# The place of the conditioning blocks in the first feed-forward stage, and who scales the last result

## What is computed

```python
def swiglu(x, w_gate_up, w_down):
    gate, up = jnp.split(x @ w_gate_up, 2, axis=-1)
    return (jax.nn.silu(gate) * up) @ w_down

# first block, for each of two layers
x = x + 0.5 * swiglu(rms_norm(x, ffn1_norm[l]), ffn1_w_gate_up[l], ffn1_w_down[l])
...                                      # three mixers
x = x + 0.5 * swiglu(rms_norm(x, ffn2_norm[l]), ffn2_w_gate_up[l], ffn2_w_down[l])

# second block
mod = silu(c) @ w_ada[l] + b_ada[l]      # 1024 x 6144, the conditioning
...
x = x + gt2 * ((silu(gte) * val) @ w_down[l])
return rmsnorm(x, g_final)
```

## Time and profile before

| what | value |
|---|---|
| time, median of 3 runs | 1635.75 us (1634.82 to 1635.97) |
| profiled execution, its own time | 1637.86 us |
| its span, first to last instruction | 1635.9 us |
| PE busy | 1583.6 us, 97% of the span |
| DVE, ACT, POOL busy | 80%, 62%, 24% |
| chain that ended last | PE 76%, DVE 13%, ACT 6%, DMA 2%, issue 2% |
| mean granted clock of PE | 0.98 of full speed |

### The profile page before, as it was taken

The page is one execution under the profiler, slowest core; times in us unless marked ns, Lnnn a source line. Parts: engine busy times, 40 slices in busy tenths (PEclk is TensorE's granted clock), DMA queues, the critical chain, the costliest instruction groups (busy, mean ns, idle before and its releaser), DMA issues.

```text
span 1635.9 us, 33829 instructions
## 1 busy us (share of the span) xinstructions
PE 1583.6 (97%) x14144; PEld 1452.6 (89%) x14144; DVE 1304.3 (80%) x2149; ACT 1011.4 (62%) x1852; POOL 394.6 (24%) x304
## 2 busy tenths in 40 slices
PE   9999998999999999999999899999999999889997
PEld 7888998988898888888899898889888899889987
DVE  6888678977868886788767997876987677889964
ACT  5775458667457764677445877646775557566742
POOL 1674000000106740277200000011773100211110
PEclk9999999999899999999999999899999999989998
DMA  7675643512266656566563341245665643245442
GB/s 270 248 267 187 217 137 92 148 49 80 104 249 235 232 202 209 205 260 225 193 227 97 112 122 36 80 155 205 236 259 178 217 161 141 104 155 185 177 160 97
DMA packets 97128, 282.77 MB, mean 173 GB/s; under 512 B 7760, under 2 KB 61648, under 8 KB 73936
## 3 DMA queue, kind: packets, MB, share of 16 engines
q1 hardware_dynamic: 96256, 279.48, 48.5%
q10 hardware_dynamic: 720, 1.13, 0.2%
HBM read 279.53 MB, written 1.05 MB: 172 GB/s over the span
## 4 chain that ended last, share of the span: by engine, by line
PE 76%; DVE 13%; ACT 6%; DMA 2%; issue 2%; POOL 0%; ACTq 0%; DVEq 0%; POOLq 0%
PE banks L516 25%; PE banks L517 13%; PE banks L508 7%; PE banks L509 7%; PE banks L510 7%; PE banks L1836 3%; DVE WL L479 3%; PE banks L1188 2%; PE banks L1190 2%; PE banks L1189 2%; DMA ring<-wst 2%; ACT ring L800 1%; ACT WH L474 1%; PE banks L1845 1%; DVE ringr L1143 1%
## 5 line engine op out<-in xcount | busy, mean ns | idle before, releaser
L479 DVE TENSOR_TENSOR WL<-ring,WH 128x2048 fp32r<-128x2048 f32 (+1 forms) x218 | 457.6, 2110 | 103.6 <-ACT WH L474 103.5
L516 PE MATMUL banks<-XNP,WH 128*128 128x512 f32 x1408 | 496.1, 396 | 3.4 <-DVE XNP L610 2.2
L474 ACT ACTIVATE WH<-ring 128x2048 fp32r<-128x2048 f32 (+1 forms) x222 | 378.7, 1714 | 46.1 <-PE banks L510 40.2
L517 PE MATMUL banks<-XNP,WL 128*128 128x256 f32 x1408 | 393.3, 279 | 0.0
L516 PEld LDWEIGHTS banks<-XNP,WH 128*128 128x128 f32 x1408 | 264.0, 187 | 64.5 <-DVE XNP L610 3.3
L1029 POOL TENSOR_TENSOR HP<-G,HP 128x256 fp32r<-128x256 f32 x110 | 210.4, 1913 | 300.9 <-ACT HP L820 300.9
L516 PE MATMUL banks<-HP,WH 128*128 128x512 f32 x770 | 269.1, 394 | 2.6 <-DVE G L932 1.8
L517 PEld LDWEIGHTS banks<-XNP,WL 128*128 128x128 f32 x1408 | 265.6, 189 | 0.0
L517 PE MATMUL banks<-HP,WL 128*128 128x256 f32 x770 | 215.9, 280 | 0.0
L516 PEld LDWEIGHTS banks<-HP,WH 128*128 128x128 f32 x770 | 145.3, 189 | 35.6 <-DVE G L932 2.1
L517 PEld LDWEIGHTS banks<-HP,WL 128*128 128x128 f32 x770 | 145.3, 189 | 0.0
(11 more groups left out here) (543 smaller groups left out, 4031.7 us busy)
## 6 DMA issues: line engine op xcount, KB each, us to landing
ring<-wst SPq DMA_DIRECT2D x179, 1024.0 KB, 4.9
ring<-wst SPq DMA_DIRECT2D x80, 704.0 KB, 4.0
ring<-wst SPq DMA_DIRECT2D x108, 256.0 KB, 2.9
LP<-lp SPq DMA_DIRECT2D x1, 1872.0 KB, 7.1
LP<-lp SPq DMA_DIRECT2D x4, 448.0 KB, 5.7
X<-xin ACTq DMA_DIRECT2D x4, 256.0 KB, 7.9
out<-X SPq DMA_DIRECT2D x4, 256.0 KB, 2.2
C<-cst SPq DMA_DIRECT2D x1, 193.0 KB, 4.8
```

Source lines behind the costliest of these rows:

```text
L474: e.do.activation(WH[:, slot[q], 0:n], ring[:, slot_at(i), 0:n], ACT.Copy).then_inc(*w_act.up("high", q))
L479: e.do.tensor_tensor(WL[:, slot[q], 0:n], ring[:, slot_at(i), 0:n], WH[:, slot[q], 0:n].bitcast(F32), ALU.subtract).then_inc(*w_dve.up("lo ...
L516: e.do.matmul(b[:, :], WH[:, s, cols], x.rearrange("p s t -> p (s t)"), start=first, stop=False)
L517: return e.do.matmul(b[:, 0:T], WL[:, s, cols], x[:, 0, :], start=False, stop=last)
```

## The change

The last three conditioning blocks of stage 0 stand behind the tiles 15, 17 and 19 instead of 16, 19 and 21. All loads behind them in the list shift accordingly, as do ACT's and POOL's steps for these blocks (steps 12, 14, 16 instead of 13, 16, 18), PE's transposes and DVE's sums; no sum of stage 0 is left in the down part. In stage 4 ACT writes each finished tile, scaled with the final scale, into `X` behind its square, and DVE forms the result from that in four instructions of two tiles each instead of eight of one tile, each behind a wait for ACT's scaled tiles.

```diff
 def ada_up(f):
-    return (7, 10, 13, 16, 19, 21) if f == 0 else (5, 8, 11, 14, 17, 20)
+    return (7, 10, 13, 15, 17, 19) if f == 0 else (5, 8, 11, 14, 17, 20)
...
                         e.do.activation(SQ[:, n % 2, :], src[:, n, :], ACT.Square).then_inc(*f_act.up("sq", f, n))
+                        if f == 4:
+                            e.do.activation(X[:, n, :], X2[:, n, :], ACT.Copy, scale=spc("gfin", n)).then_inc(*f_act.up("scaled", n))
...
             e.wait_ge(*b_pe.on("rows", "end"))
-            for k in range(KT):
-                e.do.scalar_tensor_tensor(X[:, k, :], X2[:, k, :], spc("gfin", k), bank[7][:, 0:T], ALU.mult, ALU.mult).then_inc(*b_dve.up("result", k))
+            for k in range(0, KT, 2):
+                e.wait_ge(*f_act.on("scaled", k + 1))
+                e.do.tensor_tensor(X[:, k:k + 2, :], X[:, k:k + 2, :], bank[7][:, 0:T].unsqueeze(1).to_broadcast([128, 2, T]), ALU.mult).then_inc(
+                    *b_dve.up("result", k + 1))
```

## The result

| what | before | after |
|---|---|---|
| median, runs of both in turn | 1635.8 us (20 runs) | 1637.84 us (20 runs, 1634.92 to 1640.82) |
| ratio after / before | | 1.0013, 95% interval 1.0007 to 1.0019 |
| profiled execution, its own time | 1637.86 us | 1636.07 us |
| its span | 1635.9 us | 1633.8 us |

The account below looks back on a forecast made before the run. PE, busy 97% of the span, was taken as the bound. 1637.86 + 1.1 (moved blocks) - 0.6 (result) gave 1638.4 us of own time; the +0.5 us carried to the median gave 1636.2 us, range 1634.2 to 1638.9.

Parts of the forecast that it names:

- What bounds it: Whole kernel: PE is busy 97% of the span; stage 0's stall and slow clock before the down part hold 3.5 us.
- the loops: Stage 0, blocks 2 to 5: three slot loops of 13.33 us against 11.48 us of PE work, 4.4 us of stalls.
- Part 1: Moved blocks in stage 0: down part 2.79 us later, less 1.7 us of slow clock, so +1.1 us.
- Part 2: Result at the kernel's end: four products in 2.49 us instead of 3.22, gaining 0.2 to 0.73 us, taken as 0.6.
- carrying the difference over to the median: Whole kernel: the +0.5 us found against the profiled execution was added to the timed runs' median, giving 1636.2 us.
- The sum: Whole kernel: 1637.86 + 1.1 - 0.6 = 1638.4 us of the profiled execution's own time, +0.5 us.
- The first rival: Stage 0: slow clock loss no longer hidden, or absent from earlier timed runs; 1.7 us added, 1637.9 us; 22%.
- Works as said: Stage 0 and end: blocks end earlier, PE never waits, stall and slow clock gone, end shorter; 1631.6 us; 8%.
- Loads of 7.01 us: Stage 0: three conditioning loads take 7.01 us instead of 4.84, each loop grows by 2.17; 1642.7 us; 7%.

Follow-up runs that it names:

- e3: The changed kernel with only 64 of 2048 columns loaded for conditioning blocks 3 to 5 of stage 0; 1638.22 us in one execution.
- e1: The changed kernel with the result formed as before, so only the blocks of stage 0 moved; 1640.51 us, ratio 1.0017 to the kernel before.
- e2: The changed kernel with the blocks of stage 0 placed as before, so only the new result form; 1636.59 us, ratio 0.9998 to the kernel before.
- e11: The changed kernel with the blocks of stage 0 behind tiles 7, 9, 12, 15, 18, 21; 1636.57 us, ratio 0.9997 to the kernel before.
- before_again: The kernel before, unchanged, profiled once more for its trace; stage 0 took 187.22 us.
- e10: The changed kernel with the blocks of stage 0 behind tiles 6, 9, 12, 15, 18, 21; 1636.49 us, ratio 0.9995 to the kernel before.
- e8: The changed kernel with ACT's block scaling ahead of tanh and hidden-value rounding in steps 12, 14, 16 of stage 0; 1644.65 us in one execution.

## Why the prediction was right or wrong

**What bounds it, and the loops: right in the numbers, half right in the reason.** Forecast for the scalings of blocks 3 to 5: 93.59, 106.92, 120.25; seen 93.48, 106.69, 119.89. Forecast for the waits 0.74 + 1.85 + 1.85 = 4.44 us; seen 1.15 + 1.42 + 1.62 = 4.2. Down part forecast at 141.96, seen at 141.75. But ACT didn't stand idle for the loads of blocks 4 and 5. Two loops of one length ran beside each other (block 4's load landed less than 0.1 us before its scaling began), and I had priced one. e3 shows that the other gives 13.1 us by itself. In the forecast this did no harm, because they are equal; whoever had mended the loads on its strength would have gained little.

**Part 1 against the profiled execution: right.** Forecast +1.1 us; stage 0 took 188.84 against 187.82, +1.0.

**Part 2: right.** Forecast -0.6; the four products take 2.48 us (forecast 2.49), the stores land after 2.4 us instead of 2.2, and the way from the last square to the end is about 0.5 us shorter. The Trainium skill (VectorE: DVE Perf Modes, The TRN2 errata — SBUF-src ops pay a fixed extra latency per instruction) would put a product at an estimated 658 ns, four at 2.63 us, a gain of 0.59 us (not the 0.56 of the prediction). The trace has 0.68 us for one product and 2.48 for four, since each starts 0.60 us behind the one before, and the row was the better guide. The scaled copies are hidden, the last one ending at 1625.41, 3 us ahead of the products.

**The step that failed: carrying the difference over to the median.** "That execution lies 2.1 us above the median of the timed runs, so I carry the difference of +0.5 us over to the median." The sum credited the change with 1.7 us of slow clock that would no longer be lost. The earlier trace rows were read rightly, but they were one execution, and three of four traces of this stage don't lose it. Against those three (mean 186.97 us) the changed stage 0 is 1.9 us longer, and with 0.5 us back from part 2 the sum is +1.4; the measurement says 2.0 (1.1 to 3.1). The first rival named this condition ("the timed runs of before were without the drop that the profile shows") and its time, 1637.9, against 1637.84 measured. It came out so close partly by luck: without the drop before gains not 1.7 us but about 0.85 (187.82 - 186.97), because the wait of 1.1 us for POOL in the down part, which no row of the first profile could show, then takes some of it back (the first wait differs between the traces as well, 0.8 to 1.8 us). That the timed runs are mostly without the drop is inferred: three of four traces lack it, and the timed runs, which have no trace, have a mean granted clock of 0.983 (median of the 27 beside e1 and e2) where the profiled execution has 0.980, which doesn't say where the clock fell. The 0.6 us between the sum and the measurement are open and within its interval.

The hint stood there: the profiled execution's own time was 2.1 us above the median. I wrote that down and still used a loss seen in it alone.

**The other rivals.** "Works as said" (1631.6) fell with the loops. Loads of 7.01 us didn't come in after: the three landed 4.7 to 4.9 us after their issue. But such loads do come where distances are three tiles (e11), so the mechanism was real at another place.

## What to carry to other kernels

Before crediting an edit with a stall, look at more than one trace of the kernel before: a slow clock in one execution is neither sure to return nor free of cover, since it can hide the next wait. When a loop's length fits one chain of waits, look at what the timeline puts ahead of the repeating instruction; here two chains of 13 us ran side by side, and mending either alone gave little or did harm. Moving work earlier in a ring costs where the distances become shorter than the loop, and at the start where the work isn't ready yet.

## What the runs showed of the hardware that was not expected

Three up tiles of stage 0 take PE different times, though its list of waits names none among them. Stretches between two pairs of transposes, at granted clock 1.00, in before_again and in e10:

```profile
108.71:125.20 16.49, 16.49 (x97) 14.41 (x96) 14.15 (x15) 12.52 (x20) 11.84 (x7) 1.00 0.66 235
```

```profile
104.04:121.20 17.16, 17.05 (x97) 14.82 (x97) 14.78 (x17) 11.97 (x21) 11.69 (x8) 1.00 0.70 243
```

That is 0.67 us more for as much work, and e10 has it twice. Half of it is a wait after all, of the weight loads (PEld). These are listed apart from PE's matmuls, and in e10 they wait twice for DVE's low weights, 0.35 us before tile 16 and 0.30 before tile 19, while in before_again they don't wait here:

```profile
PEld banks L516 <- DVE WL L479: 0.7, 2, 0.3
```

Of such a wait only 0.11 us shows as idle time of PE in the stretch, because PE still has the transposes in hand; but the first matmul starts 0.49 us behind them (104.15) instead of 0.14. So in e10 the low weights come a little late even at distances of three tiles. The other half is a rhythm: in PE's timeline the pairs of matmuls follow each other at some 353 ns on average in this stretch of e10, at 347 in before_again, which makes 0.3 us over three tiles. Both rhythms occur in the traces of before as well (its three tiles take 16.87 or 17.18 us with their transposes). What sets the rhythm was not tried. Added up over stage 0, the slower pairs cost between 0.4 and 1.6 us in the thirteen traces (0.9 in before_again, 1.4 in e10), so it moves the stage by up to about 1 us, as much as half of the difference that was to be explained.

A wait of a given length doesn't decide the clock by itself. In e8 PE waited 0.81 + 1.71 us close together, between 117.4 and 120.4, and the clock stayed at 1.00 behind them; it waited 0.90 + 1.71 us at the next such place and the clock fell to the lower level (0.50, from 135.6):

```profile
120.40:135.00 14.60, 11.99 (x67) 9.96 (x67) 11.67 (x12) 9.33 (x16) 8.14 (x7) 1.00 0.58 222
...
135.57:138.99 3.42, 3.42 (x13) 2.83 (x12) 3.35 (x5) 2.26 (x4) 1.35 (x1) 0.50 0.72 264
```

In before the clock fell behind a wait of 1.82 us; in after it didn't behind 1.42 and 1.62 us.
